# One contiguous row per partition for every weight, and the expert gather moved in the order of units

## The reference, cut to what matters

```python
def hier_moe(h, w_group, b_group, w_expert, b_expert, w1, w3, w2):
    g_prob = softmax(hf @ w_group + b_group)          # 8 groups, the best one is taken
    e_sel  = (hf @ w_expert + b_expert)[own group]    # 8 experts in it, the best two
    ...
    def expert_block(args):
        xb, e = args
        return (jax.nn.silu(xb @ w1[e]) * (xb @ w3[e])) @ w2[e]
```

## Time and profile before

| | |
|---|---|
| median of 3 runs | 1990.06 us (1989.99 to 1992.44) |
| the profiled execution | 1990.96 us, of which 1989.0 us are the span from its first to its last instruction |
| busy share of the span | PE 92%, PE weight load 80%, DVE 75%, ACT 61%, POOL 7% |
| DVE line 2012 (low half of an expert unit, 192 of them) | 848.5 us, 4436 ns each |
| ACT line 1560 (high half, 182 of them) | 660.9 us, 3632 ns each |
| moved by DMA | 544.11 MB in 95187 packets, mean 274 GB/s |

### The profile page before, as it was taken

The page is one execution under the profiler, slowest core; times in us unless marked ns, Lnnn a source line. Parts: engine busy times, 40 slices in busy tenths (PEclk is TensorE's granted clock), DMA queues, the critical chain, the costliest instruction groups (busy, mean ns, idle before and its releaser), DMA issues.

```text
span 1989.0 us, 26314 instructions
## 1 busy us (share of the span) xinstructions
PE 1823.6 (92%) x10364; PEld 1590.4 (80%) x10364; DVE 1483.8 (75%) x1181; ACT 1217.1 (61%) x954; POOL 131.9 (7%) x136
## 2 busy tenths in 40 slices
PE   6997899989899979989599999999999999999997
PEld 6976799989799979968577778777787777877775
DVE  5767445568545564365599898998989989899897
ACT  4454334433333344443397887878878788788885
POOL 1245000000000000440200000000000000000000
PEclk9997999999999989979599999999989999899899
DMA  7420354453345544325199999999999999999994
GB/s 259 179 85 0 128 182 179 180 235 145 127 162 187 190 180 175 122 95 212 53 405 421 388 421 385 420 422 377 421 381 420 422 376 422 382 421 422 374 421 169
DMA packets 95187, 544.11 MB, mean 274 GB/s; under 512 B 6048, under 2 KB 6176, under 8 KB 77472
## 3 DMA queue, kind: packets, MB, share of 16 engines
q1 hardware_dynamic: 95136, 543.39, 68.2%
HBM read 542.32 MB, written 1.05 MB: 273 GB/s over the span
## 4 chain that ended last, share of the span: by engine, by line
PE 58%; DVE 18%; issue 13%; ACT 9%; POOL 2%; DMA 0%; DVEq 0%; ACTq 0%; POOLq 0%; SPq 0%
PE psum L908 13%; DVE ring_r L2012 11%; PE psum L782 9%; PE psum L1224 7%; ACT arena_r L1560 7%; PE psum L918 6%; PE psum L1195 5%; PE psum L817 4%; PE psum L1209 4%; PE psum L1234 3%; PE psum L800 2%; PE psum L1160 1%; PE psum L876 1%; DVE x L2097 1%; PE psum L853 1%
## 5 line engine op out<-in xcount | busy, mean ns | idle before, releaser
L2012 DVE TENSOR_TENSOR ring_r<-ring,arena_r 128x4096 fp32r<-128x4096 f32 x192 | 848.5, 4436 | 44.2 <-ACT arena_r L1560 39.9
L1560 ACT ACTIVATE arena_r<-ring 128x4096 fp32r<-128x4096 f32 x182 | 660.9, 3632 | 16.6 <-PE psum L1224 16.6
L1195 PE MATMUL psum<-arena_r,stream_r 128*128 128x512 f32 x1024 | 412.4, 403 | 30.2 <-DVE ring_r L2012 28.9
L1195 PE MATMUL psum<-ring_r,stream_r 128*128 128x512 f32 x1024 | 401.6, 392 | 0.0
L1195 PEld LDWEIGHTS psum<-arena_r,stream_r 128*128 128x128 f32 x1024 | 193.4, 189 | 87.9 <-DVE ring_r L2012 21.6
L1779 DVE TENSOR_TENSOR ring_r<-ring,arena_r 128x3072 fp32r<-128x3072 f32 x40 | 134.3, 3358 | 160.1 <-ACT arena_r L1380 160.1
L1380 ACT ACTIVATE arena_r<-ring 128x3072 fp32r<-128x3072 f32 x40 | 110.9, 2773 | 192.4 <-DMA ring<-in_down 192.4
L1195 PEld LDWEIGHTS psum<-ring_r,stream_r 128*128 128x128 f32 x1024 | 193.4, 189 | 38.0
L908 PE MATMUL psum<-stream_r,arena_r 128*128 128x256 f32 x704 | 200.7, 285 | 6.2 <-DVE arena_r L1652 6.2
L908 PE MATMUL psum<-arena_r 128*128 128x256 f32 x704 | 200.5, 285 | 0.0
L908 PE MATMUL psum<-stream_r,ring_r 128*128 128x256 f32 x704 | 200.4, 285 | 0.0
(11 more groups left out here) (297 smaller groups left out, 2623.0 us busy)
## 6 DMA issues: line engine op xcount, KB each, us to landing
ring<-in_w SPq DMA_DIRECT2D x192, 2048.0 KB, 10.5
ring<-in_gate SPq DMA_DIRECT2D x44, 512.0 KB, 3.5
ring<-in_up SPq DMA_DIRECT2D x44, 512.0 KB, 4.4
ring<-in_down SPq DMA_DIRECT2D x44, 512.0 KB, 5.3
ring<-in_w_in SPq DMA_DIRECT2D x8, 2048.0 KB, 8.3
ring<-in_in_w SPq DMA_DIRECT2D x7, 2048.0 KB, 14.0
ring<-in_out_w SPq DMA_DIRECT2D x7, 2048.0 KB, 7.8
ring<-in_l_in SPq DMA_DIRECT2D x8, 1536.0 KB, 8.1
```

The lines of the kernel that those rows point to most:

```text
L1195: last = mm(dst, xg[:, k, :], b[:, k * D_EXPERT:(k + 1) * D_EXPERT], start=(k == 0 and b is u_hi), stop=(k == KD - 1 and b is u_lo))
L1560: A(w_hi[:, u % HI_SLOTS, :], ring[:, MOE_SLOT[at], :], ACT.Copy).then_inc(m_hi, 1)
L2012: V.tensor_tensor(ring_r[MOE_SLOT[u % NM]][:, :], raw, w_hi[:, u % HI_SLOTS, :].bitcast(F32), ALU.subtract).then_inc(m_lo, 1)
```

## The change

It changes the layout of every weight in DRAM, the order of the model dimension on the partitions, and two places in the order of units.

- Every unit lies in DRAM as 128 rows, one contiguous row for each partition (16 KB for a full one, 12 KB in the feed-forward layers). Each unit takes one DMA where the feed-forward ones took three and `kv` two.
- The model dimension is `k*128+p`: partition p holds channels p, 128+p and so on. Norm gains, the router's weights and the weights of all layers follow. In the norms' transposes and in the gather the 128 channels of a chunk now lie side by side.
- PE gathers after unit 19 in place of unit 20, so ahead of unit 20 and of the fold of expert 7. ACT and DVE do their `gathered` in step 22 in place of step 20.

```diff
-        SEND_AT, SELT_AT, SELECT_AT, GATHER_AT = 1, 3, 8, 20
+        SEND_AT, SELT_AT, SELECT_AT, GATHER_AT, GATHERED_AT = 1, 3, 8, 19, 22
...
-                W.add(f"ffn{n}_{j}", 3, release, slot)
+                W.add(f"ffn{n}_{j}", 1, release, slot)
...
             def columns(name, w, n=512):
-                load(name, (slot8(W.slot(name), n), w.rearrange("(p k) n -> p k n", k=KD)))
+                load(name, (ring[:, W.slot(name), 0:KD * n], w))
...
-                        for dst, src in pieces(FFN_SLOT[n][b], i * FFN_RING + b):
-                            sp.dma_start(dst, src).then_inc(landed[FFN_SLOT[n][b]], 16)
+                        sp.dma_start(ring[:, FFN_SLOT[n][b], 0:FFN_WORDS],
+                                     w[bass.ds(i * FFN_RING + b, 1)].rearrange("a p n -> p (a n)")).then_inc(landed[FFN_SLOT[n][b]], 16)
...
-                if kind == "w2":
-                    dst, src = unit_rows_at(slot), d["w2"][bass.ds(e * NE, NE)].rearrange("k p n -> p k n")
-                else:
-                    dst, src = ring[:, slot, :], d[kind][bass.ds(e, 1)].rearrange("a p n -> p (a n)")
-                sp.dma_start(dst, src).then_inc(landed[slot], 16)
+                sp.dma_start(ring[:, slot, :], d[kind][bass.ds(e, 1)].rearrange("a p n -> p (a n)")).then_inc(landed[slot], 16)
...
-                            last = nc.tensor.transpose(bank(f"norm{n}_{j}")[:, at:at + P], xn[:, tc, 2 * j + kk::KD], ident)
+                            last = nc.tensor.transpose(bank(f"norm{n}_{j}")[:, at:at + P], xn[:, tc, (2 * j + kk) * P:(2 * j + kk + 1) * P], ident)
...
-                        last = mm(psum[:, XG_BANK, k * CAP:(k + 1) * CAP], xn[:, tc, k::KD], sel_g[:, tc, 0:CAP],
+                        last = mm(psum[:, XG_BANK, k * CAP:(k + 1) * CAP], xn[:, tc, k * P:(k + 1) * P], sel_g[:, tc, 0:CAP],
...
-                        act.wait_ge(landed[slot], i * (16 * 3) + W.landed(f"ffn{n}_{nxt}")[1])
+                        act.wait_ge(landed[slot], i * 16 + W.landed(f"ffn{n}_{nxt}")[1])
...
-                        if u == GATHER_AT:
+                        if u == GATHERED_AT:
                             with act.If(g < N_GROUPS - 1):
                                 gathered(n + 1)
...
-                        if u == GATHER_AT:
+                        if u == GATHERED_AT:
                             with dve.If(g < N_GROUPS - 1):
                                 gathered(n + 1)
```

More of the change, by code:

```diff
@@ L517, in program @@
                                    ("z1", "z11", 512, None)):
-            W.add(n, 2 if n == "kv" else 1, O.ready(last))
+            W.add(n, 1, O.ready(last))
             if width:
@@ L575, in program @@
         NM = len(MOE)
-        def slot8(s, n=512):
-            return ring[:, s, 0:KD * n].rearrange("p (k n) -> p k n", k=KD)
         def bank(name):
@@ L628, in columns, with ffn @@
             def columns(name, w, n=512):
-                load(name, (slot8(W.slot(name), n), w.rearrange("(p k) n -> p k n", k=KD)))
+                load(name, (ring[:, W.slot(name), 0:KD * n], w))
             def rows(name, w, n):
                 for i in range(n):
[L633 to L639, removed]
+                    load(f"{name}w{i}", (ring[:, W.slot(f"{name}w{i}"), :], w[i]))
+            def ffn(n, w):
                 for j in range(FFN_RING):
-                    load(f"ffn{n}_{j}", *pieces(FFN_SLOT[n][j], j))
+                    load(f"ffn{n}_{j}", (ring[:, FFN_SLOT[n][j], 0:FFN_WORDS], w[j]))
                 with sp.Fori(1, NF // FFN_RING) as i:
@@ L646, in ffn @@
                         sp.wait_ge(ffn_part, i * FFN_RING + (n * (NF - 1) + b - FFN_RING + 1))
-                        for dst, src in pieces(FFN_SLOT[n][b], i * FFN_RING + b):
-                            sp.dma_start(dst, src).then_inc(landed[FFN_SLOT[n][b]], 16)
+                        sp.dma_start(ring[:, FFN_SLOT[n][b], 0:FFN_WORDS],
+                                     w[bass.ds(i * FFN_RING + b, 1)].rearrange("a p n -> p (a n)")).then_inc(landed[FFN_SLOT[n][b]], 16)
                 for j in range(NF // FFN_RING * FFN_RING, NF):
-                    load(f"ffn{n}_{j}", *pieces(FFN_SLOT[n][j % FFN_RING], j))
-            in_w = d["in_w"]
+                    load(f"ffn{n}_{j}", (ring[:, FFN_SLOT[n][j % FFN_RING], 0:FFN_WORDS], w[j]))
             columns("misc", d["misc"], N_MISC)
             sp.dma_start(small[:, N_FIRST:], d["small"][:, N_FIRST:]).then_inc(small_in, 16)
-            columns("iq", in_w[:, 768:1280])
-            columns("q", in_w[:, 0:512])
-            columns("xb0", in_w[:, 2376:2888])
+            columns("iq", d["in_w"][0])
+            columns("q", d["in_w"][1])
+            columns("xb0", d["in_w"][2])
             s = W.slot("kv")
-            load("kv", (ring[:, s, 0:1024].rearrange("p (k n) -> p k n", k=2), d["w_uk"].rearrange("(k p) n -> p k n", p=P)),
-                 (ring[:, s, 1024:2048].rearrange("p (k n) -> p k n", k=2), d["w_uv"].rearrange("(k p) n -> p k n", p=P)))
+            load("kv", (ring[:, s, 0:2048], d["kv_up"]))
             for i in (1, 2):
-                columns(f"xb{i}", in_w[:, 2376 + 512 * i:2888 + 512 * i])
+                columns(f"xb{i}", d["in_w"][2 + i])
             for i in range(2):
-                columns(f"z{i}", in_w[:, 1352 + 512 * i:1864 + 512 * i])
+                columns(f"z{i}", d["in_w"][5 + i])
             sp.dma_start(pos[:, :], d["positions"]).then_inc(router_in, 16)
-            sp.dma_start(w_router[:, :, :], d["w_router"].rearrange("(p k) n -> p k n", k=KD)).then_inc(router_in, 16)
+            sp.dma_start(w_router[:, :, :], d["w_router"]).then_inc(router_in, 16)
             rows("out0", d["out_w0"], 3)
-            ffn(0, d["gate0"], d["up0"], d["down0"])
+            ffn(0, d["ffn0"])
             for j in range(KD):
@@ L674, in _ @@
             sp.dma_start(norm_row[:, :], d["final_norm"].to_broadcast([P, D])).then_inc(row_in, 16)
[L675 to L679, removed]
+            ffn(1, d["ffn1"])
+            columns("fq", d["w_in2"][0])
+            columns("fk", d["w_in2"][1])
+            columns("fv", d["w_in2"][2])
             columns("misc2", d["misc2"], 264)
-            columns("sq", w2[:, 1544:2056])
+            columns("sq", d["w_in2"][3])
             for i in range(2):
-                columns(f"gf{i}", w2[:, 2312 + 512 * i:2824 + 512 * i])
+                columns(f"gf{i}", d["w_in2"][4 + i])
             for i in range(2):
-                columns(f"gs{i}", w2[:, 3336 + 512 * i:3848 + 512 * i])
-            load("pf", (unit_rows("pf"), d["proj_fox"].rearrange("(k p) n -> p k n", p=P)))
-            load("ps", (unit_rows("ps"), d["proj_swa"].rearrange("(k p) n -> p k n", p=P)))
+                columns(f"gs{i}", d["w_in2"][6 + i])
+            load("pf", (ring[:, W.slot("pf"), :], d["proj"][0]))
+            load("ps", (ring[:, W.slot("ps"), :], d["proj"][1]))
             rows("out2", d["out_w2"], 2)
@@ L2259, in _, with by_partition, ffn_units, units @@
             norm("last")
-IN_NAMES = ["small", "x", "positions", "w_router", "in_w", "misc", "w_uk", "w_uv", "out_w0", "gate0", "up0", "down0",
-            "l1_in", "out_w1", "gate1", "up1", "down1", "final_norm", "w_in2", "misc2", "proj_fox", "proj_swa", "out_w2",
+IN_NAMES = ["small", "x", "positions", "w_router", "in_w", "misc", "kv_up", "out_w0", "ffn0",
+            "l1_in", "out_w1", "ffn1", "final_norm", "w_in2", "misc2", "proj", "out_w2",
             "moe_norm", "final_norm2", "w1", "w3", "w2"]
 def layout(i):
+    def by_partition(w):
+        return w.reshape(-1, P, w.shape[-1]).transpose(1, 0, 2).reshape(P, -1)
     def chunked(w):
-        return w.reshape(P, KD, -1, P).transpose(2, 0, 1, 3)
+        return w.reshape(KD, P, NF, P).transpose(2, 1, 0, 3).reshape(NF, P, KD * P)
+    def ffn_units(gate, up, down):
+        return np.concatenate([chunked(gate), chunked(up), down.reshape(NF, P, D)], axis=2)
+    def units(w, starts):
+        return np.stack([by_partition(w[:, a:a + 512]) for a in starts])
+    def row_units(w):
+        return np.stack([by_partition(w[a:a + 512]) for a in range(0, w.shape[0], 512)])
+    def experts(w):
+        return w.reshape(N_EXPERTS, -1, P, w.shape[-1]).transpose(0, 2, 1, 3).reshape(N_EXPERTS, P, SLOT)
     def all_rows(v):
@@ L2287, in layout @@
         "half": np.full((P, 8), -0.5),
-        "attn_norm": i["l0_attn_norm"].reshape(P, KD), "ffn_norm": i["l0_ffn_norm"].reshape(P, KD),
-        "l1_norm": i["l1_conv_norm"].reshape(P, KD), "ffn1_norm": i["l1_ffn_norm"].reshape(P, KD),
-        "attn2_norm": i["attn_norm_2"].reshape(P, KD), "moe_norm": i["ffn_norm_2"].reshape(P, KD),
+        "attn_norm": chan(i["l0_attn_norm"]), "ffn_norm": chan(i["l0_ffn_norm"]),
+        "l1_norm": chan(i["l1_conv_norm"]), "ffn1_norm": chan(i["l1_ffn_norm"]),
+        "attn2_norm": chan(i["attn_norm_2"]), "moe_norm": chan(i["ffn_norm_2"]),
         "kv_norm": chan(i["l0_kv_norm"]),
@@ L2307, in layout @@
```

(23 more changed lines are left out.)

6 lines of the change are left out of this document (1 added, 5 removed).

## The result

The changed kernel takes 1959.85 us (median of four runs, 1958.56 to 1960.66) against 1991.25 us for the kernel before beside it; the ratio is 0.9842, 95% interval 0.9825 to 0.9859. The gain is 31.4 us; 24 were forecast. The profiled execution took 1959.51 us, 1957.7 of them the span.

What follows compares the result with a forecast made beforehand. PE bounds the feed-forward stage; in the expert stage waits count, 7.8 us a group on DVE around the gather. -28.7 + 4.1 + 2 - 0.4 - 1.0 = -24 us from 1990.06 gives 1966 us, range 1951 to 1986.

Steps and rivals of the forecast that it cites:

- Part 1: Expert-stage gather: without the step of 8 floats, 3.5 us at the full clock where it took 7.65; 6.9 at half.
- Part 2: Transposes of the six norms, at a clock of 0.50: gain from side-by-side data taken as 0, at most 7 us.
- Part 3: New order in an expert group: DVE's idle time 3.7 us instead of 7.8, gaining 4.1 a group, 28.7 over seven.
- Part 4: PE's clock in the new gathers: falls in one of seven, giving back 4.1 us; bounds none and all seven.
- Part 5: Weight loads: 427 GB/s with 16 KB rows, only cover in the expert stage; late landings 2 us, first load gains 0.4.
- late landings: Expert loads landing after ACT needs them: 0 to 1 us a group, taken at 0.3, 2 us in all.
- The first load: `misc`, 1.67 MB, with ACT waiting for it: 4.3 to 3.9 us, a gain of 0.4 (bounds 0 and 1).
- the two terms that did not come: Losses in the expert stage: 4.1 us for one clock fall in seven groups, 2 us for loads landing late.

## Why the prediction was right, and where it was off

The time, 1959.85 us, lies inside 1951 to 1986 and 6 us below the 1966 forecast.

- **Part 1 held.** 3.52 us at the full clock (3.5 forecast), 7.10 at half the clock (6.9 forecast). The one access put back gave 7.6 us and cost all of the gain. The rule of the Trainium skill ("SBUF — State Buffer", the note on cachelines in the section on the port swizzle), that an access pays where each element falls into another line, is borne out for this gather at the full clock: 239 against 110 ns a record.
- **Part 2 held.** The 16 transposes of a norm have the same median of 421 ns as before, and the piece of ten in the chain is 2.38 us both times. At a clock of 0.50 the step costs the transposes nothing; whether it would at 1.00 no run shows.
- **Part 3 held**, to tenths: DVE's waits are 3.6 us (3.7 forecast), the period 120.35 (120.3 forecast). The seven groups give 7 x 4.1 = 28.7 us, the largest term. What the text did not say, and what follows from the same working, is that the new place is a loss: with the short gather the old place gives 119.16 us a group. The change is a layout worth 37 us (1991.97 to 1954.86) and a move that gives back 5 of them.
- **Part 4 is the term that was mis-sized.** I gave back 4.1 us for one fall of the clock in seven groups; there was none. The price was too high as well: the two gathers of like length above put a fall at about 2 us (unit 20 at 5.43 in place of 3.79, and slower gates), not at the whole gain of a group. I took the length of the run of small matmuls as the cause, as it fell 3.2 to 6.7 us into it by my reading (3.5 to 6.6 by the table in half us). The doubled gather, 7.5 us of them without a fall, shows that the length was not it; the strided gather at the same place shows the fall again.
- **Part 5 held for the bound**: 16 KB rows move 428 to 429 GB/s where the share is 1.01 (the groups of the gather after unit 21). The forecast has 427; its own rows, 422 over a mix with a third at 408, give 429, and nothing in the sum hangs on that. The loads were cover, and `w2` in short rows changes nothing at this order. The 2 us that I gave for late landings did not come (no wait for an expert's load, at most 13.4 us to landing). The first load lands 0.1 us earlier, not 0.4; why so little no run shows. The rule of 512 bytes of the Trainium skill ("DMA: Bandwidth & Descriptors", Specifications), by which rows of 2, 4 and 16 KB would be alike, is not borne out: 395, 422 and 429 GB/s with rows of 2 and 4, of 4 and 16, and of 16 KB. Short rows for all expert weights made the loads the bound and cost the changed kernel 58 us.
- Without the two terms that did not come the sum is -28.7 - 0.4 - 1.0 = -30.1 us, against -31.4 measured. The remaining 1.3 us I did not follow. The changed kernel and its three other orders are the same up to the expert stage, and yet it begins at 978.2 to 983.4 us (first gather) in their profiles, so 1.3 us is below what one profile can tell.

## What to carry to other kernels

Where a tensor is TensorE's stationary operand, lay the 128 columns side by side: a step of 8 floats more than doubled each float32 record of the gather at the full clock (239 against 110 ns), and it also brought the clock down, which the unit behind it paid. Before moving a step in an order by hand, list who stands behind it on its own engine; against the old place behind unit 20, the gather ahead of the fold cost 5 us with the new layout and 12 with the old one; behind unit 21, where almost nothing waited for it, it gained 11 (1954.86 to 1944.03, with its rounding two steps later). A longer row in DRAM is worth its price only from the point at which the loads are the bound; compare bytes over the measured rate with the period of the loop first.

## What the runs showed of the hardware that I had not expected

- A run of small float32 matmuls (64 columns, a weight load each) did not bring the granted clock down here: 1.00 over 7.5 us, 111 ns a record. The same 32 records with a step of 8 floats in the weights, 239 ns each, were followed by 0.50 in each gather of the kernel before. Whether the step acts by making the array wait is argued, not shown; shown is that the step decides and the length does not.
- The strided gather has the same pace at both clocks (6 records a us), the contiguous one about half the pace at half the clock (3.52 and 7.10 us for the same 32 records).
- The DMA engines show a share of 1.04 at 395 GB/s and of 1.01 at 429: the share alone does not say how well they move.
